# A decoder step's last expert tile: u rows gathered token by token, x spread by TensorE, v 16 tokens behind

## What is computed

```python
act = gelu(einsum('thkd,td->thk', u_tab[idx], xb))
ff = einsum('thk,thkd->td', gate * act, v_tab[idx])
out = layer_norm(ALPHA * x + ff, ln2_g, ln2_b)
```

## Time and profile before

| what | value |
|---|---|
| runs (us) | 5211.97, 5188.72, 5198.52; median 5198.52 |
| profiled execution | 5198.58 us, its span 5196.8 us |
| mean granted TensorE clock | 0.802 |
| share of the span busy: PE, DVE, POOL, ACT | 66%, 64%, 52%, 14% |
| the last stage | from 4873 us to the end of the span |
| DMA in it | 217 GB/s in the u half, 369 GB/s in the v half |

### The profile page before, as it was taken

One profiled execution on the slowest core, in us unless ns is written; L12 is line 12 of the kernel. 1 busy time (PEld: TensorE's weight loads), 2 busy tenths in 40 slices (PEclk: granted clock), 3 DMA queues, 4 the chain that ended last, 5 costly groups with the idle time before them and its releaser, 6 DMA issues. The chain is left out here.

```text
span 5196.8 us, 52661 instructions
## 1 busy us (share of the span) xinstructions
PE 3423.1 (66%) x17388; PEld 1932.9 (37%) x17388; DVE 3351.0 (64%) x7219; ACT 726.6 (14%) x2591; POOL 2704.2 (52%) x2288
## 2 busy tenths in 40 slices
PE   7887466699785666566499977467566536656206
PEld 6574352354551541442244463163154113211001
DVE  4345896578535985786577543797687657785480
ACT  2131210111310210200122121110111010000000
POOL 1000566466433775774365534466676565426676
PEclk9998678799887778778699988787777765578658
DMA  5543678899766889999799757789998986759768
GB/s 192 170 143 114 216 239 323 295 401 351 286 243 251 318 311 372 352 322 354 273 352 333 287 212 291 292 278 346 377 337 322 356 307 221 279 205 386 262 222 332
DMA packets 467260, 1497.00 MB, mean 288 GB/s; under 512 B 60096, under 2 KB 122240, under 8 KB 454416
## 3 DMA queue, kind: packets, MB, share of 16 engines
q0 software_dynamic: 324864, 1141.04, 59.6%
q1 hardware_dynamic: 120912, 330.01, 17.2%
q10 hardware_dynamic: 21216, 22.60, 1.3%
HBM read 1480.07 MB, written 55.29 MB: 295 GB/s over the span
## 5 line engine op out<-in xcount | busy, mean ns | idle before, releaser
L2027 POOL DMA_INDIRECT e_ring<-peer_u,e_idx x1152 | 1458.7, 1266 | 1090.9 <-issue 526.6
L2027 POOL DMA_INDIRECT e_ring<-peer_v,e_idxT x1104 | 1196.5, 1084 | 1025.2 <-PE e_ff L2179 509.8
L2063 DVE CUSTOM_DVE_ANT_0 e_ring<-e_ring,e_x 128x1024 f32<-128x1024 f32 (+1 forms) x1152 | 1380.4, 1231 | 302.6 <-DMA e_ring<-peer_u,e_idx 294.8
L2179 PE MATMUL e_ff<-e_ring,e_strips 128*32 128x512 f32 x4416 | 726.3, 756 | 611.8 <-DMA e_ring<-peer_v,e_idxT 500.9
L351 PE MATMUL p_ps<-p_hT,p_w 128*128 128x256 f32 (+2 forms) x1728 | 567.6, 483 | 0.0
L2179 PEld LDWEIGHTS e_ff<-e_ring,e_strips 128*32 128x32 f32 x4416 | 163.8, 126 | 1066.9 <-issue 1065.1
L351 PEld LDWEIGHTS p_ps<-p_hT,p_w 128*128 128x128 f32 x1728 | 327.6, 195 | 208.1 <-issue 129.5
L1314 PE MATMUL bank<-wbuf,kqb 128*128 128x512 f32 (+1 forms) x544 | 278.1, 666 | 101.3 <-DMA wbuf<-w_out 101.1
L1400 PE MATMUL bank<-wbuf,kqb 128*128 128x512 f32 (+1 forms) x576 | 275.5, 628 | 21.5 <-DMA wbuf<-wc 21.5
L375 PE MATMUL p_ps<-p_w,p_hT 128*128 128x512 f32 (+1 forms) x576 | 253.5, 603 | 0.0
L1816 DVE MAX8 top<-kb_kdec 128x8 f32<-128x128 f32 (+1 forms) x144 | 40.3, 280 | 330.2 <-ACT kb_kdec L1541 330.2
(11 more groups left out here) (334 smaller groups left out, 4446.1 us busy)
## 6 DMA issues: line engine op xcount, KB each, us to landing
p_w<-w_in SPq DMA_DIRECT2D x156, 512.0 KB, 7.4
wbuf<-w_out SPq DMA_DIRECT2D x72, 1024.0 KB, 9.5
wbuf<-wc SPq DMA_DIRECT2D x72, 1024.0 KB, 8.1
e_ring<-peer_u,e_idx POOLq DMA_INDIRECT x1152, 6.3
e_ring<-peer_v,e_idxT POOLq DMA_INDIRECT x1104, 6.8
rows<-p_tok SPq DMA_DIRECT2D x72, 192.0 KB, 8.2
rows<-rows SPq DMA_DIRECT2D x8, 1280.0 KB, 8.9
z<-p_zs SPq DMA_DIRECT2D x32, 256.0 KB, 6.3
```

The costliest lines, as they stand in the source:

```text
L2027: g.indirect_dma_start(out=self.ring[:, i % RING, :], out_offset=None, in_=table[:, :], in_offset=at, bounds_check=NEXP - 1, oob_is_err=Fa ...
L2063: v.tensor_tensor_reduce(out=self.ring[0:U, i, :], in0=self.ring[0:U, i, :], in1=self.x[0:U, :], scale=1.0, scalar=0.0, op0=ALU.mult, op1= ...
L2179: last = nc.tensor.matmul(self.ff[i][32 * j:32 * j + 32, :], self.strips[:, self.strip_of[t] % NSTRIP, j, 31 - s:63 - s], self.ring[:, sel ...
```

## The change

Only the last tile changes. `experts_by_token` takes the place of `experts_alone`. The u rows are now gathered token by token, 128 slots on the partitions, with the same turned indices as v: 80 gathers of 128 rows. The dot then needs the token's x on every partition: TensorE makes that copy with a column of the identity broadcast to 128 columns (`copies`), into one of two PSUM buffers `spread`, and VectorE reads x from there. The results stand already turned, so the gates are turned once at the start and no transpose of `dots` is left. Gelu and weights are done for 8 tokens at a time. The sequence of gathers is u(0) to u(15), then u(16), v(0), u(17), v(1) and so on, and v(64) to v(79) at the end (LAG = 16). Ring, batch of four and the v matmuls stay. The first gather waits for `idx_taken`. The end (layer norm, stores) is the same.

```diff
--- before.py
+++ after.py
@@ -745,6 +745,7 @@
 RING = 12
 BATCH = 4
 NSTRIP, STRIP = 2, 63
+LAG, GROUP = 16, 8
 GELU = ((0, 112), (112, SLOTS))
 NW = 2
 LEVELS, LEVELS_PACK = 7, 4
@@ -2219,46 +2220,155 @@
             sp.wait_ge(self.S["y_out"], 16 * sum(len(self.outputs(tile)) for tile in self.y_tiles))
 
 
-def experts_alone(nc, e, pool_dma):
+def experts_by_token(nc, e, pool_dma):
 
     ctx = ExitStack()
     with ctx:
-        S = Signals(nc, ctx, e.names, pool_dma)
-        e.begin(nc, ctx, S)
+        names = ["turned", "idx_taken", "gate_taken", "spread", "dot", "act_done", "weight", "strip", "v_used", "ff_init", "gathered",
+                 "chain", "ff_read", "y_pre", "y_out"]
+        S = Signals(nc, ctx, names, pool_dma)
+        io, B, R = e.io, e.B, PACK
+        order = lane_order(R)
+        seq = []
+        for i in range(R + LAG):
+            seq += [("u", i)] * (i < R) + [("v", i - LAG)] * (i >= LAG)
+        at_seq = {entry: g for g, entry in enumerate(seq)}
+        firsts = [m for m in range(R) if m == 0 or order[m][1] != order[m - 1][1]]
+        strip_of = [sum(1 for f in firsts if f <= m) - 1 for m in range(R)]
+        width = [strip_of.count(q) for q in range(len(firsts))]
         turn = [ctx.enter_context(nc.psum_tensor(f"turn{i}", [P, 512], F32, allow_name_mangling=True)) for i in range(2)]
+        spread = [ctx.enter_context(nc.psum_tensor(f"spread{i}", [P, D], F32, allow_name_mangling=True)) for i in range(2)]
+        idxT, dots, gates = e.idxT_of(LAST), e.dots, e.wT
+        row = lambda kind, n: e.ring[:, at_seq[kind, n] % RING, :]
+        def landed(eng, kind, n):
+            g = at_seq[kind, n]
+            eng.wait_ge(S[f"in{g % RING}"], 16 * (g // RING + 1))
         with nc.Block() as block:
             @block.gpsimd
             def _(g):
-                at = e.pool(g)
-                e.pool_end(g)
+                off = lambda n: bass.IndirectOffsetOnAxis(ap=idxT[:, 32 * order[n][0] + order[n][1]:32 * order[n][0] + order[n][1] + 1], axis=0)
+                g.wait_ge(S["idx_taken"], 1)
+                for i, (kind, n) in enumerate(seq):
+                    if i >= RING:
+                        was, m = seq[i - RING]
+                        if was == "u":
+                            g.wait_ge(S["dot"], m + 1)
+                        else:
+                            g.wait_ge(S["v_used"], m // BATCH + 1)
+                    g.indirect_dma_start(out=row(kind, n), out_offset=None, in_=io["peer_u" if kind == "u" else "peer_v"][:, :],
+                                         in_offset=off(n), bounds_check=NEXP - 1, oob_is_err=False).then_inc(S[f"in{i % RING}"], 16)
+                for i in range(RING):
+                    g.wait_ge(S[f"in{i}"], 16 * len(range(i, len(seq), RING)))
+                g.sem_inc(S["gathered"], 1)
+                nums = [S[f"in{i}"].num for i in range(RING)]
+                g.dma_reset(range(min(nums), max(nums) + 1))
 
             @block.tensor
             def _(pe):
-                at = e.tensor(pe)
-                e.tensor_start(pe, turn[0])
-                at("rows")
-                e.tensor_turn(pe, turn[1])
-                e.tensor_end(pe)
+                ident, mm = B["ident"], nc.tensor.matmul
+                nc.tensor.transpose(turn[0][:, 0:P], e.idx_f[:], ident[:, :])
+                nc.tensor.transpose(turn[1][:, 0:P], e.gate[:], ident[:, :]).then_inc(S["turned"], 1)
+                def copies(n):
+                    if n >= 2:
+                        pe.wait_ge(S["dot"], n - 1)
+                    t = 32 * order[n][0] + order[n][1]
+                    for i in range(2):
+                        last = mm(spread[n % 2][:, i * 512:(i + 1) * 512], ident[0:R, t:t + 1].to_broadcast([R, P]),
+                                  e.x[0:R, i * 512:(i + 1) * 512], start=True, stop=True)
+                    last.then_inc(S["spread"], 1)
+                copies(0)
+                copies(1)
+                for i in range(2):
+                    last = mm(e.ff[i][:, :], e.alpha[:], e.x[:, i * 512:(i + 1) * 512], start=True, stop=False, skip_group_check=True)
+                last.then_inc(S["ff_init"], 1)
+                for kind, n in seq:
+                    if kind == "u" and n + 2 < R:
+                        copies(n + 2)
+                    if kind == "v" and n % BATCH == BATCH - 1:
+                        some = range(n - BATCH + 1, n + 1)
+                        for m in some:
+                            landed(pe, "v", m)
+                        pe.wait_ge(S["strip"], strip_of[n] + 1)
+                        for i in range(2):
+                            for m in some:
+                                j, s = order[m]
+                                last = mm(e.ff[i][32 * j:32 * j + 32, :], e.strips[:, strip_of[m] % NSTRIP, j, 31 - s:63 - s],
+                                          row("v", m)[:, i * 512:(i + 1) * 512], start=False, stop=(s == 31), skip_group_check=True)
+                        last.then_inc(S["v_used"], 1)
 
             @block.scalar
             def _(act):
-                at = e.scalar(act)
-                at("rows")
-                e.scalar_turn(act, turn[1])
-                e.scalar_end(act)
+                act.wait_ge(S["turned"], 1)
+                by_lane = turn[1][:, 0:P].rearrange("p (j s) -> p s j", s=32)
+                nc.scalar.copy(gates[:, 0:48].rearrange("p (s j) -> p s j", j=3), by_lane[:, 0:16, 0:3])
+                nc.scalar.copy(gates[:, 48:R].rearrange("p (s j) -> p s j", j=2), by_lane[:, 16:32, 0:2]).then_inc(S["gate_taken"], 1)
+                for kind, n in seq:
+                    if kind == "u" and n % GROUP == GROUP - 1:
+                        sl = slice(n + 1 - GROUP, n + 1)
+                        act.wait_ge(S["dot"], n + 1)
+                        nc.scalar.activation(dots[:, sl], dots[:, sl], ACT.Gelu).then_inc(S["act_done"], 1)
+                    if kind == "v" and n in firsts:
+                        q = strip_of[n]
+                        act.wait_ge(S["weight"], (n + width[q] - 1) // GROUP + 1)
+                        if q >= NSTRIP:
+                            act.wait_ge(S["v_used"], (firsts[q - NSTRIP + 1] - 1) // BATCH + 1)
+                        nc.scalar.copy(e.strips[:, q % NSTRIP, 0:width[q], 31:32],
+                                       dots[:, n:n + width[q]].unsqueeze(2)).then_inc(S["strip"], 1)
 
             @block.vector
             def _(v):
-                at = e.vector(v)
-                e.vector_mid(v)
-                e.vector_start(v, turn[0])
-                at("rows")
-                e.vector_turn(v)
-                e.vector_end(v)
+                c = Chain(v, S["chain"])
+                v.wait_ge(S["turned"], 1)
+                v.tensor_copy(idxT, turn[0][:, 0:P]).then_inc(S["idx_taken"], 1)
+                def weigh(b):
+                    sl = slice(b * GROUP, (b + 1) * GROUP)
+                    if b == 0:
+                        v.wait_ge(S["gate_taken"], 1)
+                    v.wait_ge(S["act_done"], b + 1)
+                    v.tensor_tensor(dots[:, sl], dots[:, sl], gates[:, sl], ALU.mult).then_inc(S["weight"], 1)
+                for n in range(R):
+                    landed(v, "u", n)
+                    v.wait_ge(S["spread"], n + 1)
+                    v.tensor_tensor_reduce(out=row("u", n), in0=row("u", n), in1=spread[n % 2][:, :], scale=1.0, scalar=0.0,
+                                           op0=ALU.mult, op1=ALU.add, accum_out=dots[:, n:n + 1]).then_inc(S["dot"], 1)
+                    if n % GROUP == 0 and n >= GROUP:
+                        weigh(n // GROUP - 1)
+                weigh(R // GROUP - 1)
...
+                inverse_root(v, c, e.root[0:R, :], e.root_x[0:R, :], e.root_w[0:R, :], e.mv[0:R, 1:2], 1.0, LN_EPS)
+                v.wait_ge(S["ff_read"], 1)
+                v.scalar_tensor_tensor(out=y, in0=y, scalar=e.root[0:R, 0:1], in1=e.bias[0:R, :], op0=ALU.mult,
+                                       op1=ALU.add).then_inc(S["y_pre"], 1)
 
             @block.sync
             def _(sp):
-                e.sync(sp)
+                outs = e.outputs(LAST)
+                sp.wait_ge(S["y_pre"], 1)
+                for dst, some in outs:
+                    sp.dma_start(dst, e.ring[some, 0, :]).then_inc(S["y_out"], 16)
+                sp.wait_ge(S["y_out"], 16 * len(outs))
         nc.all_engine_barrier(sems_to_clear=S.range)
 
 
@@ -2303,8 +2413,7 @@
         mix(6, u=5, head=(5, 0, 80))
         mix(7, tail=(5, 80, P), u=6, head=(6, 0, 64))
         mix(LAST, tail=(6, 64, P), u=7, head=(7, 0, P))
-        e.bind(io, B, {"mid": (0, 0, 0), "rows": (0, 1, 0), "tokens": (0, 0, 1)}, u=LAST, head=(LAST, 0, PACK))
-        experts_alone(nc, e, pool_dma)
+        experts_by_token(nc, e, pool_dma)
         store_states(nc, io, B)
```

(17 more changed lines are left out.)

## The result

The changed kernel took 5226.15 us (median; 5214.64 to 5232.66), the kernel before 5199.11 us beside it (5184.97 to 5211.97): ratio 1.0051, 95% interval 1.0035 to 1.0067. So it is half a per cent slower, and 4 us above the upper end of the range. In the two profiled executions (5224.28 and 5198.58 us) 5.4 us of the difference of 25.7 lie ahead of the last stage, in code that is the same in both. The last stage, from the first matmul that turns the indices to the end of the last ff matmul, went from 305.9 to 326.1 us. That is the change's part: 20.2 us more. "Stage" means this stretch from here on.

The account below looks back on a forecast made before the run. No engine reached 70% busy; a loop of waits over ring and batch would bound the changed stage. Head to 4920, 14 periods (217 us) and end (38.1) finish at 5175.1 instead of 5179.6: 5194 us, own range 5181 to 5210, 8-in-10 range 5168 to 5222.

Parts of the forecast that it names:

- stage start to the end of batch 0: Opening of the last stage: TensorE the bound at 1.71 us a token, first v batch ending at 4920.
- loop without falls: Waits from one v batch's end to the next, through slot release, gathers, dot, copies and batch: 14.07 us at full clock.
- falls per gap: How often TensorE's clock grant falls in the 3.5 us idle gap of each period: five times in six.
- cost of one fall: Time lost when TensorE's clock falls to 1.2 GHz in a gap: 1.7 us.
- period: Four tokens of the loop, from one batch's end to the next: 14.07 + 0.83 x 1.7 = 15.5 us.
- 14 periods: Middle of the last stage, batches ending with tokens 7 to 59: 14 x 15.5 = 217 us, to 5137.
- end: Last v batches after the loop, from v(63) to v(79): 38.1 us, TensorE ending at 5175.1.
- landing of u(m+23): In the loop, issue to landing of the u gather second after POOL's pause: 5.3 us, bounds 4.2 and 6.5.
- rival 4: In the loop, the dot blocks the gather after all: 0.9 us a period, 13 in all, time 5207; chance 0.05.
- the slow rival: In the loop, late u landings plus a long low clock: period 17.7 us, time 5227; chance 0.1.
- Rival 3: In the loop, landing 6.5 us, low clock 4.8 us after each gap costing 2.4: period 17.7, time 5227; chance 0.1.
- The head: Stage start to first batch: low clock until about 4885, token 21's copies end at 4916.5, batch 0 at 4920.

Follow-up runs that it names:

- e3_filled: Changed kernel with three extra fp32 identity matmuls filling TensorE's gap in each period, ahead of the waiting copies; ratio 0.9991, stage 314.3 us.
- e1_batch2: Changed kernel with v batches of two tokens instead of four in the last stage; ratio 0.9906, stage 271.2 us.
- e4_ring24: Changed kernel with a ring of 24 slots instead of 12 for the last stage, batch of four kept; ratio 0.9934, stage 275.8 us.
- e7_rows128: Changed kernel with only the copies multiplying over 128 rows instead of 80, same output; ratio 1.0020.
- e2_lag80: Changed kernel with v 80 tokens behind u instead of 16, so all u gathers come first; ratio 1.0141, stage 383.3 us.
- e6_lag80_rows128: Changed kernel with v 80 tokens behind u instead of 16 and copies over 128 rows instead of 80; ratio 0.9908, stage 263.8 us.
- e8_all3: Changed kernel with batches of two, a ring of 24 slots and copies over 128 rows together; ratio 0.9879, stage 260.3 us.

## Why the prediction was wrong

The table follows the prediction's steps (us; the measured column is from the changed kernel's trace).

| step | predicted | measured |
|---|---|---|
| stage start to the end of batch 0 | 46.3 | 48.95 |
| loop without falls | 14.07 | 14.2 (e3_filled) |
| falls per gap | 5 of 6 | 14 of 14 |
| cost of one fall | 1.7 | 2.8 |
| period | 15.5 | 16.98 |
| 14 periods | 217 | 237.7 |
| end | 38.1 | 39.4 |

**The loop was right, term by term.** POOL's 0.80 us, the issue of 1.3, the landing of u(m+23) at 5.1 to 5.8 for 5.3 taken, 1.28 for dot and step, 1.71 + 3.63 at full clock: e3_filled gives the sum back at 14.2. That the slot of v(m) and the order of TensorE's queue close it is shown by opening it at either place (e1_batch2, e4_ring24). That gathers take 0.99 us beside dots with x in PSUM was right (rival 4 is out), and so was where POOL, TensorE and VectorE would stand idle.

**What failed is the size of a fall of the clock.** I took 1.7 us from the earlier trace rows, a batch in which the grant fell 0.2 us after TensorE began and came back 3.6 us after it, and had a second row in hand, 4.8 us, which I kept for the slow rival. In the changed kernel the fall came before TensorE began again (1.3 us before, in the period shown) and the grant was back 5.5 us after it: 5.5 us at half the clock, 2.8 us lost, which is also the difference to e3_filled. And it fell in each gap and not in five of six. The 80 rows are not the reason: with 128 (e7_rows128) the period is the same. Per period that is 2.8 - 0.83 x 1.7 = 1.4 us, 20 us in all, of the 24.7 us by which the stage missed my sum. Rival 3 had the right part (its 2.4 us for the clock) beside a wrong one (a landing of 6.5 us; the median of u's landings in the loop is 6.3, but the row on the loop's path, second after POOL's pause, came in 5.1 to 5.8). Clock as in rival 3 and landing as in mine gives 14.07 + 2.4 = 16.5 a period, 5208 us, and the full 2.8 us in each gap 16.9, 5213: both still inside the range. What carried the time out of it is small beside that: 2.6 us of head, 1.3 us of end, and 5.4 us ahead of the stage, which belong to no step; with 1.2 us more in the loop beside the falls they give the 5224 us of the profiled execution, and the median is 2 us above it.

**The head was late by 2.6 us by a slip in my sum.** The low clock at its start was right: I had it end at about 4885, 11.3 us after TensorE began, and it ended after 11.1. But from there to the end of token 21's copies are twenty tokens, 20 x 1.71 = 34.2 us, which ends at 4919.2 and not at 4916.5; the trace has the 80 matmul records of these tokens in 34.70 us. The 80-row copies that fill the head cost time there all the same (the runs with 128 rows have the grant back after 2.8 to 5.9 us), but I had counted that time in without knowing its cause. **The end was late by 1.3 us**: its first batch took 6.31 us where I had 5.4, again the larger price of a fall; two batches later 0.5 us of that was left, and the rest came with the later landing of the last v rows.

The Trainium skill, page "TensorE: Matmul & The Clock Gate", section "Part 1: The HAM clock gate", says that the grant follows how busy TensorE has been lately. The traces agree for the falls and for work on 128 rows. They don't for the copies on 80 rows of e2_lag80, at 1.2 GHz over 236 us with TensorE busy for 235.3 of them. Here the measurement decides.

## What to carry to other kernels

Where an in-order queue reuses slots that are freed in batches, write down the loop from one release to the next with every landing in it: here batches of two instead of four, or a ring of 24 slots instead of 12, turned a ratio of 1.0051 into 0.9906 and 0.9934. A gap in each period of such a loop can cost TensorE's clock as well, and its price is to be taken from the longest rise that the traces show and not from the shortest; here even the longest, at 2.4 us, was under the 2.8 measured. And where a stream of matmuls on fewer rows stays at 1.2 GHz although TensorE is busy, try it on all 128 rows with zero weights in the rest: the outputs here stay the same and the instructions take as long.

## What was not expected of the hardware

- fp32 matmuls of 512 columns over 80 rows held a grant of 1.00 (4949.8 to 4963.4 in e2_lag80) and never raised one of 0.50 (236 us at 99.7% busy). Over 128 rows, with the same one-column weights, the grant was back after 6.8 us (e6_lag80_rows128, on another chip). At the same clock both take the same time (copies of a token 1.7 us at 1.00).
- After a fall in the loop the grant was low for 6.8 us with either width; after TensorE's start in the stage it was low for 9.5 to 11.3 us with 80 rows (six runs) and for 2.8 to 5.9 us with 128 (six runs), on one chip 10.0 against 3.5 to 5.7. Why the loop doesn't feel the rows is open.
- On the slower chips dots at the start of the stage waited for rows of u, with 24 slots 4.2 to 7.2 us each for four of them in a row, although 411 GB/s moved (e8_all3), and TensorE was busy for only 13 of 30 us. With 12 slots the waits were fewer and shorter; on the third chip, with 12 slots or paced, they weren't seen. The cause is open.
